# Out-projections chunk by chunk over each group of units in a two-layer mLSTM and gMLP trunk

## The chip, the cores and the metric

The kernel runs on the 8 cores of one Trainium2 chip. Two cores share a sequence of the batch: the even one takes the first 17 units of 128 tokens, the odd one the last 15. Time is device microseconds of the slowest core, the median of several executions. TensorE multiplies, VectorE (DVE), ScalarE (ACT) and GpSimd (POOL) do the rest, SyncE (SP) issues DMAs, as do ACT and POOL.

## The reference

`reference` runs two layers over x of shape (4, 4096, 2048), each with a residual add, and a last RMSNorm:

```python
xn = rmsnorm(h, mlstm_norm_g);  h = h + mlstm_layer(xn, ...)   # y @ w_out, y 4096 wide
xn = rmsnorm(h, gmlp_norm_g);   h = h + gmlp_layer(xn, ...)    # y @ w_out, y 4096 wide
return rmsnorm(h, final_norm_g)
```

The mLSTM layer projects to q, k, v, two gates and more, runs a chunked scan over 8 heads, norms and gates the result; the gMLP layer mixes tokens within chunks of 128. Both end in a product of (tokens x 4096) with (4096 x 2048), the out-projection, which is what the change touches.

## The kernel before

An even core (`PASSES_E`) takes its 17 units in passes of n = 9 and 8. An odd core (`PASSES_O`) first builds the scan's state out of the even core's tokens (`prefix`), then takes its 15 units in passes of 8 and 7. A pass is `phase_a` (projections, scan, by head), `phase_b` (out-projection `w0`, with the second layer's norm), `phase_cd` (gMLP up to the gate) and `phase_e` (out-projection `w1`, with the final norm, and with the first norm of the next pass's units among it).

**Weights.** `WQ` (class at L199 and on) has 5 slots (`NWSLOT`) of one chunk each: 8 x 128 rows by 512 columns, cast to bf16 by the DMA, which GpSimd issues (L218). `cur` hands out the slots of the next chunks, `done(k)` lets go of k chunks in their order, and each time issues the load of the next chunk that has none yet, that is five chunks further on. The issue waits on GpSimd's queue until TensorE has read the slot. An input projection takes 2 chunks (K = 2048), an out-projection 4 per column block `cb` (K = 4096), and there are 4 blocks of 512 columns.

**Order.** The code is written out in program order; each engine keeps to it. `sc.tick()` advances a counter, and `sc.defer(k, f)` has f written out at the k-th tick from now. A tick is thus a place in the order of TensorE's work, not a time.

**Out-projection** (`out_phase`). The units are split in g0 and g1 (4 and 4 for n = 8, 4 and 3 for n = 7). For each block and group, each unit of the group gets a PSUM bank out of a ring of 6 (`accr`) and the 16 matmuls of chunks 0 and 1; then each gets the 16 of chunks 2 and 3 and its `evict`. There is a tick behind every 16 matmuls. In g1 `done(2)` stands between the halves and again at the end. In blocks 0 to 2 `evict` adds the residual's tile (L1313; 5 tiles, loaded 4 ahead by SP), ScalarE squares it with a sum (L1286) and issues its DMA to `h_scr`. In block 3 the add (L1297) goes into a row of 2048 (4 rows in `w0`, 5 in `w1`), which `load_row` fills from `h_scr` and the residual in two DMAs (L193 and L1274), and then follow square, reduce (L1301), `rstd` on GpSimd (L509, L512) and `finish`.

`finish` of `phase_b` writes the row's last quarter to `h_scr`, defers `norm_scale` (L538, VectorE) by one tick and `norm_T` by three: 16 transposes on TensorE (L546) into banks PT and PS, which ScalarE (L551) and VectorE (L554) copy out. `finish` of `phase_e` defers the scale (L1509) and the row's output DMA by one. The row of unit s + 4 (or s + 5) is loaded a few ticks behind unit s's `evict`. `phase_cd` needs unit s's transposed norm at its projection of unit s (L649), `phase_a` starts with L631.

Of the kernel before, what the change touches and what calls it, by code (L numbers as in the profile page):

```python
# [279 lines left out]
def build_program():  # L280
# [32 lines left out]
    def emit(res, PREFIX, PASSES):  # L313
# [3 lines left out]
        sc = Sched()  # L317
# [931 lines left out]


        def out_phase(S, n, ub, key, res, resb, orow, finish):
# [26 lines left out]
            def mmg(ws, c0, s, pj, pjb, start, stop):  # L1278
                k = len(ws)
                tk.mm([lambda p, i=i: p.matmul(pj[:, :], lhsT=S.yt[:, c0 * 8 + i, s * 128:(s + 1) * 128],  # L1280
                                               rhs=ws[i // 8][0][:, i % 8, :], start=(start and i == 0),
                                               stop=(stop and i == 8 * k - 1)) for i in range(8 * k)],
                      reads=[w[1] for w in ws] + [S.ytb[(c0 * 8 + 4 * i) // 4][s] for i in range(2 * k)], writes=[pjb])
# [8 lines left out]
            def evict(cb, s, pj, pjb):  # L1292
                u = ub + s
                if cb == 3:
# [11 lines left out]
                    if s + len(orow) < n:  # L1306
                        sc.defer(len(orow) - 1, lambda: load_row(s + len(orow)))
# [14 lines left out]
            for cb in range(4):  # L1322
# [5 lines left out]
                for gi, g in enumerate((g0, g1)):  # L1328
                    for s in g:
                        open_[s] = accr.next()  # L1330
                        mmg(ws[0:2], 0, s, open_[s][0], open_[s][1], True, False)
                        sc.tick()
                    if gi == 1:
                        wq.done(2)
                    for s in g:
                        mmg(ws[2:4], 2, s, open_[s][0], open_[s][1], False, True)
                        evict(cb, s, *open_[s])
                        sc.tick()
                wq.done(2)

        def phase_b(S, n, ub):
# [4 lines left out]
            def finish(s, r, rb, k, ss):  # L1346
# [3 lines left out]
                sc.defer(1, lambda: norm_scale(ns, (r, rb), ss, s))  # L1350
                sc.defer(3, lambda: norm_T(ns, s, S.xt, s))
# [124 lines left out]
        def phase_e(S, n, ub, nxt):  # L1476
            ns = S.ns
            ns.gain = None
            if nxt is not None:
# [10 lines left out]
                def a2(s):  # L1490
                    st[s] = (st[s], norm_sq(ns, st[s], s))
# [4 lines left out]
                for s in range(n2):  # L1496
                    sc.defer(4 * s, lambda s=s: a1(s))
                    sc.defer(4 * s + 6, lambda s=s: a2(s))
                    sc.defer(4 * s + 7, lambda s=s: a3(s))
                    sc.defer(4 * s + 10, lambda s=s: norm_T(ns, s, S2.xt, s))  # L1500
                sc.defer(4 * n2 + 7, lambda: ns.set_gain(gfbc_d))
# [3 lines left out]
            def finish(s, r, rb, k, ss):  # L1505
# [8 lines left out]
                sc.defer(1, last_)  # L1514
# [91 lines left out]
```

How the kernel before makes its waits and increments, by code:

```python
    def wait(self, e, tk):  # L137
        if tk is None:
            return
        sem, val, key = tk
        if key == e and e == "pe":
            return
        if self.seen[e].get(key, 0) >= val:
            return
        self.eng[e].wait_ge(sem, val)
        self.seen[e][key] = val
# [23 lines left out]
    def op(self, e, fn, reads=(), writes=()):  # L170
        self._deps(e, reads, writes)
        ins = fn(self.eng[e])
        self.cnt[e] += 1
        ins.then_inc(self.sem[e], 1)
        tk = (self.sem[e], self.cnt[e], e)
        self._mark(tk, reads, writes)
        return tk
# [1 line left out]
    def mm(self, fns, reads=(), writes=()):  # L179
        e = "pe"
        self._deps(e, reads, writes)
        ins = None
        for fn in fns:
            ins = fn(self.eng[e])
        self.cnt[e] += 1
        ins.then_inc(self.sem[e], 1)
        tk = (self.sem[e], self.cnt[e], e)
        self._mark(tk, reads, writes)
        return tk
# [1 line left out]
    def dma(self, e, ds, out, in_, reads=(), writes=()):  # L191
        self._deps(e, reads, writes)
        self.eng[e].dma_start(out=out, in_=in_).then_inc(ds.sem, 16)
        ds.cnt += 16
        tk = (ds.sem, ds.cnt, ds.key)
        self._mark(tk, reads, writes)
        return tk
# [12 lines left out]
    def _load(self):  # L210
# [5 lines left out]
        tk._deps("pool", (), [b])  # L216
        for (co, ncol, src) in self.chunks[i][1]:
            tk.eng["pool"].dma_start(out=t[:, :, co:co + ncol], in_=src).then_inc(ds.sem, 16)
            ds.cnt += 16
```

## Time and profile before

| | us |
|---|---|
| median of 3 executions (lowest, highest) | 4827.49 (4821.77, 5116.9) |
| profiled execution, its own time | 4821.41 |
| its span, slowest core (7) | 4817.8 |
| spans of the odd cores | 4811.4 to 4817.8 |
| spans of the even cores | 4714.0 to 4716.9 |

The 3.6 us between the profiled execution's time and its span lie around the traced instructions. A row of a timeline gives the start, the duration, engine, source line, output and inputs, count, and in brackets the idle time before it with what ended it. Rows of equal instructions are merged; a merged row of matmuls overlaps the next by the drain of its last one.

### The profile page before, as it was taken

To read this page: it belongs to the slowest core of one execution; us is meant where nothing else is said; L and a number is where in the kernel's file an instruction comes from. 1 tells how busy PE (TensorE), PEld (TensorE's weight loads), DVE (VectorE), ACT (ScalarE), POOL (GpSimd) and SP (SyncE) were. 2 spreads that over 40 slices of the span, in tenths; PEclk is the share of its full clock that TensorE was granted. 3 is DMA by queue.
4 is the path that set the end of the run, shared out by engine and by line. 5 is a ranking of instruction groups with operands and counts; after the bars stand their busy time and mean duration, and the time that the engine had idled before them with its cause. 6 is when DMAs were issued, how large, how long until landed. Compare 5 with 4: busy or idle time off the path is not lost.

```text
span 4817.8 us, 70400 instructions; the slowest of 8 cores (4714.0 to 4817.8 us)
## 1 busy us (share of the span) xinstructions
PE 4616.2 (96%) x25992; PEld 2346.1 (49%) x25992; DVE 1639.2 (34%) x2973; ACT 1484.6 (31%) x2951; POOL 602.8 (13%) x843
## 2 busy tenths in 40 slices
PE   4899989999999999999999999999999999999998
PEld 3564445555555544444444445555555444455543
DVE  5571023443333420202444224444334211044312
ACT  5451023333333320342222213444333213322200
POOL 2000011111112110100000011212112100000000
PEclk9999999999999999999999999999999999999999
DMA  9454264554555458644554797565656686555577
GB/s 267 64 110 96 54 157 64 82 82 78 73 77 82 77 118 174 128 75 71 76 79 74 186 225 133 83 91 82 93 78 80 131 181 113 88 88 83 87 132 211
DMA packets 430603, 520.59 MB, mean 108 GB/s; under 512 B 14768, under 2 KB 375600, under 8 KB 423344
## 3 DMA queue, kind: packets, MB, share of 16 engines
q0 software_dynamic: 368144, 335.63, 48.2%
q1 hardware_dynamic: 44688, 148.65, 9.2%
q10 hardware_dynamic: 17424, 31.73, 1.9%
q8 instruction: 213, 3.49, 0.3%
q14 instruction: 134, 1.10, 0.1%
HBM read 791.01 MB, written 60.56 MB: 177 GB/s over the span
## 4 chain that ended last, share of the span: by engine, by line
PE 88%; DMA 7%; issue 2%; DVE 2%; ACT 1%; POOL 0%; SPq 0%; DVEq 0%; ACTq 0%; POOLq 0%
PE ps_PJ L649 30%; PE ps_PJ L1422 17%; PE ps_PJ L631 7%; PE ps_PJ L1280 6%; PE ps_PK L1280 5%; PE ps_PK L631 4%; DMA sb_w<-w_out 4%; PE ps_PK L649 3%; PE ps_PJ L876 2%; PE ps_PN L1280 2%; PE ps_PN L631 2%; DMA sb_w<-w_in 2%; PE ps_PK L876 1%; PE ps_PN L649 1%; PE ps_PN L1099 1%
## 5 line engine op out<-in xcount | busy, mean ns | idle before, releaser
L649 PE MATMUL ps_PJ<-sb_w,sb_xnT 128*128 128x512 bf16 x6720 | 1493.4, 379 | 14.7 <-DVE sb_scr L641 14.3
L649 PEld LDWEIGHTS ps_PJ<-sb_w,sb_xnT 128*128 128x128 bf16 x6720 | 650.0, 98 | 775.5 <-issue 20.0
L1422 PE MATMUL ps_PJ<-sb_xnT,sb_w 128*128 128x512 bf16 (+1 forms) x4096 | 850.3, 366 | 0.0
L1422 PEld LDWEIGHTS ps_PJ<-sb_xnT,sb_w 128*128 128x128 bf16 x4096 | 395.5, 98 | 402.3
L218 POOL DMA_DIRECT2D sb_w<-w_in x288 | 256.3, 896 | 2379.5 <-PE ps_PJ L649 576.9
L1280 PE MATMUL ps_PJ<-sb_w,sb_YT 128*128 128x512 bf16 x1920 | 426.3, 380 | 11.5 <-DMA sb_w<-w_out 11.5
L631 PE MATMUL ps_PJ<-sb_xnT,sb_w 128*128 128x388 bf16 (+1 forms) x1920 | 295.1, 311 | 31.8 <-DMA sb_w<-w_in 31.8
L1280 PE MATMUL ps_PK<-sb_w,sb_YT 128*128 128x512 bf16 x1280 | 291.5, 386 | 18.2 <-DMA sb_w<-w_out 18.2
L1280 PEld LDWEIGHTS ps_PJ<-sb_w,sb_YT 128*128 128x128 bf16 x1920 | 187.3, 98 | 238.1 <-issue 18.3
L1286 ACT ACTIVATE sb_scr<-sb_scr 128x512 bf16<-128x512 f32 x120 | 75.5, 630 | 737.1 <-DVE sb_scr L1313 533.6
L641 DVE SCALAR_TENSOR_TENSOR sb_scr<-ps_PJ,sb_convw,sb_scr 128x384 f32<-128x384 f32 (+1 forms) x432 | 245.0, 569 | 108.4 <-ACT sb_scr L636 50.2
L631 PEld LDWEIGHTS ps_PJ<-sb_xnT,sb_w 128*128 128x128 bf16 x1920 | 186.2, 98 | 119.6 <-issue 41.3
L1280 PEld LDWEIGHTS ps_PK<-sb_w,sb_YT 128*128 128x128 bf16 x1280 | 126.0, 99 | 173.6 <-issue 30.7
L1076 DVE SCALAR_TENSOR_TENSOR sb_scr<-ps_PS,sb_bk,sb_maskT 128x128 bf16<-128x128 f32 x120 | 42.0, 350 | 471.7 <-PE ps_PT L1082 468.4
L631 PE MATMUL ps_PK<-sb_xnT,sb_w 128*128 128x388 bf16 (+1 forms) x1280 | 194.0, 306 | 7.4 <-DMA sb_w<-w_in 7.4
L1118 DVE COPY sb_dnt<-ps_PS 128x3 f32<-128x3 f32 (+1 forms) x120 | 19.3, 161 | 470.3 <-PE ps_PS L1107 443.4
L641 DVE SCALAR_TENSOR_TENSOR sb_scr<-ps_PK,sb_convw,sb_scr 128x384 f32<-128x384 f32 (+1 forms) x288 | 160.4, 561 | 50.8 <-ACT sb_scr L636 27.5
L1159 POOL TENSOR_TENSOR sb_scr<-sb_scr 128x512 f32<-128x512 f32 x120 | 143.6, 1197 | 229.3 <-ACT sb_scr L1230 224.2
L1206 ACT ACTIVATE sb_scr<-ps_PJ 128x512 bf16<-128x512 f32 x120 | 71.7, 597 | 324.2 <-PE ps_PJ L649 324.2
L1448 ACT ACTIVATE sb_scr<-ps_PJ 128x512 bf16<-128x512 f32 (+1 forms) x128 | 73.0, 571 | 300.2 <-PE ps_PJ L1422 236.4
L1123 DVE SCALAR_TENSOR_TENSOR sb_scr<-sb_scr,sb_egt,ps_PK 128x512 f32<-128x512 f32 x224 | 157.5, 744 | 18.3 <-PE ps_PK L1113 4.0
L509 POOL TENSOR_TENSOR sb_sm<-sb_sm,sb_epst 128x1 f32<-128x1 f32 x182 | 42.5, 233 | 954.7 <-ACT sb_scr L1149 515.8
(206 smaller groups left out, 4890.1 us busy)
## 6 DMA issues: line engine op xcount, KB each, us to landing
sb_w<-w_in POOLq DMA_DIRECT2D x224, 1024.0 KB, 13.4
sb_w<-w_out POOLq DMA_DIRECT2D x64, 1024.0 KB, 14.6
sb_w<-w_in POOLq DMA_DIRECT2D x64, 512.0 KB, 11.5
h_scr<-sb_scr ACTq DMA_DIRECT2D x105, 256.0 KB, 6.2
sb_scr<-h_scr SPq DMA_DIRECT2D x30, 768.0 KB, 8.1
sb_YT<-xp SPq DMA_DIRECT2D x16, 1024.0 KB, 13.5
sb_scr<-xm SPq DMA_DIRECT2D x60, 256.0 KB, 5.6
sb_scr<-h_scr SPq DMA_DIRECT2D x60, 256.0 KB, 6.8
```

Source lines behind the costliest of these rows:

```text
L218: tk.eng["pool"].dma_start(out=t[:, :, co:co + ncol], in_=src).then_inc(ds.sem, 16)
L631: tk.mm([lambda p, kc=kc: p.matmul(pj[:, 0:n + 4], lhsT=wts[kc // 8][0][:, kc % 8, c0:c0 + 128], rhs=xt.ap[:, kc, t0:t0 + n + 4], start=(k ...
L641: tk.op("dve", lambda v, j=j: v.scalar_tensor_tensor(out=acc[:, 0:n], in0=pj[:, 1 + j:1 + j + n], scalar=convw[:, ch, j:j + 1], in1=acc[:, ...
L649: tk.mm([lambda p, kc=kc: p.matmul(pj[:, :], lhsT=xt.cols(kc, s), rhs=wts[kc // 8][0][:, kc % 8, :], start=(kc == 0), stop=(kc == KC - 1)) ...
L876: tk.mm([lambda p, k=k, u=u: p.matmul(pj[:, :], lhsT=xn(u)[0][:, i * 128:(i + 1) * 128], rhs=kw[:, j, u, :], start=(start and k == 0), sto ...
L1123: tk.op("dve", lambda v, cc=cc, PK=PK: v.scalar_tensor_tensor(out=C[:, cc, :], in0=C[:, cc, :], scalar=egt[:, c, h:h + 1], in1=PK[:, :], o ...
L1159: tk.op("pool", lambda g: g.tensor_tensor(out=hz, in0=S.hg[0], in1=sz, op=ALU.mult), reads=[szb, S.hg[1]], writes=[hzb])
L1206: tk.op("act", lambda a, s=s, pj=pj: a.activation(out=S.vt[:, s, :], in_=pj[:, :], func=AF.Copy), reads=[pjb], writes=[S.vtb[s]])
L1280: tk.mm([lambda p, i=i: p.matmul(pj[:, :], lhsT=S.yt[:, c0 * 8 + i, s * 128:(s + 1) * 128], rhs=ws[i // 8][0][:, i % 8, :], start=(start a ...
L1286: tk.op("act", lambda a: a.activation(out=S.sqj[0], in_=x, func=AF.Square, scale=D ** -0.5, accum_out=S.hsq[:, s, cb:cb + 1]), reads=[xb], ...
L1422: tk.mm([lambda p, kc=kc: p.matmul(pj[:, 0:m * 128], lhsT=wts[kc // 8][0][:, kc % 8, c0:c0 + 128], rhs=xt.cols(kc, u0, m), start=(kc == 0) ...
L1448: tk.op("act", lambda a, pj=pj, szt=szt, w=w: a.activation(out=szt[:, 0:w], in_=pj[:, 0:w], func=AF.Silu), reads=[pjb], writes=[sztb])
```

## The change

The four chunks of a block are gone through one by one over the whole group, with a tick behind every 8 matmuls, and in the last group each chunk is let go of behind its last unit. In block 3 the groups come from `groups(n)`: 3, 3, 3 for n = 9, else 4 and the rest, which for n = 8 and 7 are the groups as before. Deferrals that count ticks of the out-projection are doubled (`phase_e`), or set anew: in `phase_b` the norm steps of a unit in the last group keep 1 and 3 ticks, those of the i-th unit of another group are put 4 + i and 7 + i ticks behind its `evict`; a row is loaded anew 8 (`w0`) or 10 (`w1`) ticks behind the `evict` of the unit that had it.

```diff
+        def groups(n):
+
+            k = 4 if n < 9 else 3
+            return [list(range(a, min(a + k, n))) for a in range(0, n, k)]
...
-            def mmg(ws, c0, s, pj, pjb, start, stop):
-                k = len(ws)
+            def mmg(w, c0, s, pj, pjb):
                 tk.mm([lambda p, i=i: p.matmul(pj[:, :], lhsT=S.yt[:, c0 * 8 + i, s * 128:(s + 1) * 128],
-                                               rhs=ws[i // 8][0][:, i % 8, :], start=(start and i == 0),
-                                               stop=(stop and i == 8 * k - 1)) for i in range(8 * k)],
-                      reads=[w[1] for w in ws] + [S.ytb[(c0 * 8 + 4 * i) // 4][s] for i in range(2 * k)], writes=[pjb])
+                                               rhs=w[0][:, i, :], start=(c0 == 0 and i == 0),
+                                               stop=(c0 == 3 and i == 7)) for i in range(8)],
+                      reads=[w[1], S.ytb[2 * c0][s], S.ytb[2 * c0 + 1][s]], writes=[pjb])
...
-                        sc.defer(len(orow) - 1, lambda: load_row(s + len(orow)))
+                        sc.defer(2 * len(orow), lambda: load_row(s + len(orow)))
...
-                for gi, g in enumerate((g0, g1)):
-                    for s in g:
-                        open_[s] = accr.next()
-                        mmg(ws[0:2], 0, s, open_[s][0], open_[s][1], True, False)
-                        sc.tick()
-                    if gi == 1:
-                        wq.done(2)
-                    for s in g:
-                        mmg(ws[2:4], 2, s, open_[s][0], open_[s][1], False, True)
-                        evict(cb, s, *open_[s])
-                        sc.tick()
-                wq.done(2)
+                gs = groups(n) if cb == 3 else (g0, g1)
+                for g in gs:
+                    for c0 in range(4):
+                        for s in g:
+                            if c0 == 0:
+                                open_[s] = accr.next()
+                            mmg(ws[c0], c0, s, open_[s][0], open_[s][1])
+                            if c0 == 3:
+                                evict(cb, s, *open_[s])
+                            sc.tick()
+                        if g is gs[-1]:
+                            wq.done(1)
...
-                sc.defer(1, lambda: norm_scale(ns, (r, rb), ss, s))
-                sc.defer(3, lambda: norm_T(ns, s, S.xt, s))
+                gs = groups(n)
+                d = 0 if s in gs[-1] else 2 + [g.index(s) for g in gs if s in g][0]
+                sc.defer(2 + d if d else 1, lambda: norm_scale(ns, (r, rb), ss, s))
+                sc.defer(5 + d if d else 3, lambda: norm_T(ns, s, S.xt, s))
...
-                    sc.defer(4 * s, lambda s=s: a1(s))
-                    sc.defer(4 * s + 6, lambda s=s: a2(s))
-                    sc.defer(4 * s + 7, lambda s=s: a3(s))
-                    sc.defer(4 * s + 10, lambda s=s: norm_T(ns, s, S2.xt, s))
-                sc.defer(4 * n2 + 7, lambda: ns.set_gain(gfbc_d))
+                    sc.defer(8 * s, lambda s=s: a1(s))
+                    sc.defer(8 * s + 12, lambda s=s: a2(s))
+                    sc.defer(8 * s + 14, lambda s=s: a3(s))
+                    sc.defer(8 * s + 20, lambda s=s: norm_T(ns, s, S2.xt, s))
+                sc.defer(8 * n2 + 14, lambda: ns.set_gain(gfbc_d))
...
-                sc.defer(1, last_)
+                sc.defer(2, last_)
```

## Rows read from the trace of the kernel before

**Rows 1.** Spans of the cores: us, mean granted TensorE clock.

```profile
core 6: 4715.7 us, clock 0.994
...
core 7: 4817.8 us, clock 0.991
```

**Rows 2.** Page, part 1, TensorE: busy us, share, instructions.

```profile
PE 4616.2 (96%) x25992; PEld 2346.1 (49%) x25992; DVE 1639.2 (34%) x2973; ACT 1484.6 (31%) x2951; POOL 602.8 (13%) x843
```

**Rows 3.** Waits of TensorE on core 7: us in total, times, longest.

```profile
PE ps_PT L546 <- ACT sb_xnT L551: 18.6, 8, 4.2
...
PE ps_PK L1280 <- DMA sb_w<-w_out: 18.2, 7, 6.1
...
PE ps_PJ L1280 <- DMA sb_w<-w_out: 11.5, 8, 3.0
...
PE ps_PK L631 <- DMA sb_w<-w_in: 7.4, 1, 7.4
...
PE ps_PJ L649 <- DMA sb_w<-w_in: 0.4, 1, 0.4
```

**Rows 4.** Chain of waits in `w0` of pass 1: start us, us, what.

```profile
1852.23 13.82 DMA sb_w<-w_out
```

**Rows 5.** Timeline of GpSimd, end of the first `w1` phase.

```profile
2882.57 2.70 POOL L218 DMA_DIRECT2D sb_w<-w_in  x3 [5.47 <-PE ps_PN L1280]
```

**Rows 6.** Timeline of TensorE: usual groups, and groups behind waits for weights.

```profile
1900.71 10.52 PE L1280 MATMUL ps_PJ<-sb_w,sb_YT 128*128 128x512 bf16 x48
...
1926.78 3.62 PE L1280 MATMUL ps_PN<-sb_w,sb_YT 128*128 128x512 bf16 x16
...
2736.04 8.50 PE L1280 MATMUL ps_PK<-sb_w,sb_YT 128*128 128x512 bf16 x32 [6.07 <-DMA sb_w<-w_out]
...
2903.28 6.84 PE L631 MATMUL ps_PK<-sb_xnT,sb_w 128*128 128x388 bf16 x32 [7.45 <-DMA sb_w<-w_in]
...
3456.12 2.79 PE L631 MATMUL ps_PK<-sb_xnT,sb_w 128*128 128x388 bf16 x16
...
3834.35 5.30 PE L1280 MATMUL ps_PK<-sb_w,sb_YT 128*128 128x512 bf16 x16 [3.08 <-DMA sb_w<-w_out]
...
4647.98 6.49 PE L1280 MATMUL ps_PK<-sb_w,sb_YT 128*128 128x512 bf16 x16 [5.29 <-DMA sb_w<-w_out]
...
4718.22 12.21 PE L1280 MATMUL ps_PJ<-sb_w,sb_YT 128*128 128x512 bf16 x48 [2.96 <-DMA sb_w<-w_out]
```

**Rows 7.** Page, part 6: loads by count, KB each, median us to landing.

```profile
sb_w<-w_out POOLq DMA_DIRECT2D x64, 1024.0 KB, 14.6
...
sb_scr<-h_scr SPq DMA_DIRECT2D x30, 768.0 KB, 8.1
```

**Rows 8.** Waits of TensorE, around `w0` of pass 1, then of pass 2.

```profile
PE ps_PT L546 <- ACT sb_xnT L551: 5.2, 3, 2.6
...
PE ps_PT L546 <- ACT sb_xnT L551: 3.8, 2, 2.4
```

**Rows 9.** Timeline of all engines, last group of `w0` in pass 1.

```profile
1972.87 0.68 DVE L1297 TENSOR_TENSOR sb_scr<-ps_PJ,sb_scr 128x512 f32<-128x512 f32 x1
...
1975.47 0.61 PE L546 MATMUL ps_PT<-sb_ident,sb_scr 128*128 128x128 bf16 x8 [1.97 <-ACT sb_xnT L551]
...
1975.80 2.35 DVE L538 SCALAR_TENSOR_TENSOR sb_scr<-sb_scr,sb_sm 128x2048 bf16<-128x2048 f32 x1 [0.49 <-POOL sb_sm L512]
...
1978.07 0.68 DVE L1297 TENSOR_TENSOR sb_scr<-ps_PN,sb_scr 128x512 f32<-128x512 f32 x1
```

**Rows 10.** Timeline of TensorE, first group's norms of `w0`, pass 1.

```profile
1942.41 4.24 PE L1280 MATMUL ps_PJ<-sb_w,sb_YT 128*128 128x512 bf16 x16
```

**Rows 11.** Timeline of all engines, the end of the span.

```profile
4795.87 7.07 PE L1280 MATMUL ps_PJ<-sb_w,sb_YT 128*128 128x512 bf16 x32
...
4810.14 2.35 DVE L1509 SCALAR_TENSOR_TENSOR sb_scr<-sb_scr,sb_sm 128x2048 f32<-128x2048 f32 x1 [1.20 <-POOL sb_sm L512]
```

**Rows 12.** Timeline of TensorE, `phase_a`: two matmuls into banks PK0 and PK1.

```profile
1739.07 0.59 PE L1113 MATMUL ps_PK<-sb_scr 128*128 128x512 bf16 x2
```

## The prediction

> **What bounds the kernel now.** First the cores: the odd ones, which run the state scan and then passes of 8 and 7 units, last 4811 to 4818 us, the even ones (9 and 8 units) 4714 to 4717 [rows 1]. The time is core 7's, and an even core has 100 us to spare: all counts below are of core 7. Then the page's busy times: TensorE is busy 4616.2 of 4817.8 us [rows 2], so what can be had is mostly in its 200 us of idle time and what its clock loses after waits. Then TensorE's waits [rows 3]: in the out-projections (L1280) it waits 15 times for `w_out` chunks, 18.2 + 11.5 = 29.7 us; once, at the first block after the first `w1` phase, 7.4 us for `w_in`, and 0.4 us at another phase start; 18.6 us for transposes of the norms (L546 after L551), of which those behind `w0` are 5.2 + 3.8 us [rows 8]. The chain of waits shows why a chunk is late: after a column block it runs through a DMA of 13.82 us that began when GpSimd issued it at 1852.23 [rows 4], with a second one behind it, since `done(2)` lets go of two.
>
> **The order of the matmuls and the release of slots.** One chunk and unit is 8 matmuls. Their pace is (10.52 - 3.62) / 32 = 0.2156 us [rows 6], so a step of the new order is 1.73 us where the old one was 3.45. The count of matmuls, weight loads, evictions and DMAs does not change. With 5 slots, letting go of chunk k starts the load of chunk k + 5, which for chunk c of a block is chunk c + 1 of the next. Before, chunks 0 and 1 went together, halfway through the last group: 4 x 3.45 = 13.8 us ahead of the block's end for n = 8, 3 x 3.45 = 10.4 us for n = 7, and the very first matmul of the next block wanted the late one. A `w_out` chunk takes 14.6 us to land in the median [rows 7]. So every block boundary is a few us short, which is what the 15 waits say. After, chunk 0 goes at 3/4 of the last group still to come (20.7 us for n = 8, 15.5 for n = 7) and its successor is wanted a full step row later (4 x 1.73 = 6.9 us into the next block): 27.6 and 22.5 us of lead. Chunk 2 of the next block gets 13.8 + 13.8 = 27.6 (n = 7: 10.4 + 13.8 = 24.2), chunk 3 gets 6.9 + 20.7 = 27.6 (n = 7: 5.2 + 20.7 = 25.9). The worst landing read off the waits is 13.8 + 6.1 = 19.9 us for n = 8 and 10.4 + 5.3 = 15.7 for n = 7; all leads are longer. At a phase's first block the chunk that used to be wanted 13.8 us in is now wanted 20.7 us in. Bounds: all 29.7 us go, or, if bursts of evictions and row loads push landings to 28 us, some 10 stay. I take 2 left: 27.7 gained.
>
> **The clock behind these waits.** Behind five of them the granted clock falls to its lower level for a stretch, seen as longer rows of the same count [rows 6]: 8.50 against 7.07 us for 32 matmuls, 5.30 against 3.62 and 6.49 against 3.62 for 16, 12.21 against 10.52 for 48, and at L631 6.84 where 32 matmuls of that width take 2 x 2.79 less the overlap of 0.16 that each group of 16 has with the next (3.62 against 3.45), 5.4. That is 1.4 + 1.7 + 2.9 + 1.7 + 1.4 = 9.1 us, and it goes with the waits.
>
> **The next phase's first weights.** The 7.4 us stood before chunk 1 of the first block of pass 2, issued at 2882.57 behind half of the last group, with two more transfers [rows 5], and landed at 2903.3: 20.7 us. It is now issued 20.7 us ahead of the end instead of 13.8, alone. Bounds: 6.9 us gained, or all 7.4 with less company in the queue. I take 6.9, and 0.4 at the other start, 7.3. What is queued behind a waiting release on GpSimd is `rstd` of later units; in block 3 the releases now lie between groups of evictions, and the last one still comes behind the last unit's `rstd`, as before, but holds one chunk that is wanted late, where it held two.
>
> Sum of gains: 27.7 + 9.1 + 7.3 = 44.1 us.
>
> **The norm steps in block 3 of `w0`.** One unit's chain on VectorE, from add (L1297) through ScalarE's square, reduce, GpSimd's two steps and the scale (L538, 2.35 us) to the next unit's add, takes 1978.07 - 1972.87 = 5.2 us [rows 9], because the scale is put right behind the evict and holds up the next add. TensorE's tick was 3.45 us, now it is 1.73. For the first group the scales are put off by 4 ticks and more and spaced by two (3.46 us, for a scale of 2.35 us and a short copy): its waits, 2.6 us in pass 1 and 2.4 in pass 2 [rows 8], and the clock behind them, about 1.5 us in each pass (an estimate from the row of 4.24 us where 3.62 is usual [rows 10] and the transposes ahead of it) go. For the last group the distance is unchanged in ticks and halved in time. With e the end of its first unit: the add starts at about e + 0.15, the scale ends 1975.80 + 2.35 - 1972.87 = 5.3 us later, and the first transpose can run at e + 5.6 and TensorE is there at e + 3.45: waits 2.2. The second is put behind ScalarE's copy of the first, which is behind the third unit's square; by rows 9 it comes 1975.47 - 1972.87 = 2.6 us after the third add, which is at e + 0.15 + 2 x 5.3 = e + 10.7: e + 13.3. For n = 8 TensorE is there at e + 8.2 (waits 5.1), for n = 7, one projection of the next phase later, at e + 10.0 (waits 3.3). The third in n = 8 waits 0.8, the fourth nothing. With about 2 us of clock behind each: 10.1 and 7.2 us, 17.3 together, against 9.0 of waits [rows 8] and 3 of clock now. That is 5.3 us lost. Bounds: 0 (VectorE's chain shortens, since its squares wait less) to 12 (row loads late as well: for n = 7 a row is now reloaded 5 ticks and some transposes, about 11 us, ahead of its add, and 768 KB land in 8.1 [rows 7]).
>
> **Evictions.** In blocks 0 to 2 four adds come 1.73 us apart instead of 3.45, then a pause of 20.7 us. An add is 0.68 us, a bank is wanted again five steps (8.6 us) after its last matmul, and the residual tiles of a group are loaded in the pause: hidden. If that cover went, each group would pay the excess over 8.6 us.
>
> **Phase `w1`.** Its ticks for the next pass's norms are doubled, which leaves their times where they were: 0. In block 3 the scale comes two ticks behind, so adds of two units lie closer. At the very end: TensorE ends at 4795.87 + 7.07 = 4802.9, the last scale at 4812.5 [rows 11], the span 5.3 us later. After, three units must be finished from 3.3 us before TensorE's end; a unit costs VectorE 5.2 us less the 1.20 that the scale waited for GpSimd [rows 11], now covered by the next unit's add, 4.0; so it would end 12.0 - 3.3 = 8.7 us behind TensorE, against 9.6 now. But rows 5 and 6 are reloaded 10 ticks behind their forerunners, only 4 ticks = 6.9 us before their adds, and take 8.1 [rows 7]: some 1.5 us late. Bounds -0.5 to +4; I take +1.
>
> **Sum.** -44.1 + 5.3 + 1 = -37.8 us, on a span of 4817.8 and a time of the profiled execution of 4821.4: 4783.6. The median shown, 4827.5, lies 6 above that execution, so the same gain from it gives 4789.7. I take 4787, -0.8%.
>
> **A rule weighed.** A group now goes to another PSUM bank every 8 matmuls instead of every 16, 240 more changes of bank on core 7 (30 unit-phases x 4 blocks x 2). The row of L1113 has two matmuls into two different banks, 0.59 us together [rows 12], so the second starts about 0.21 us behind the first: a change of bank costs nothing that shows.
> The Trainium skill, "TensorE: Matmul & The Clock Gate", section "A second HAM failure mode: psum-queue depth-cycling", says that cycling through banks let TensorE pause briefly between groups so often that its clock went up and down and throughput fell. By that rule this change would be slower (rival 2); the trace does not agree so far, since groups of 16 follow each other without a gap at the upper of the two levels.
>
> **Rivals.** (1) The waits move instead of going. For: DMA is shared by weights, rows, residuals and outputs, and in block 3 the rows' loads now come 1.73 us apart. Against: leads are 22 us and more. Half of 27.7 + 9.1 stays, and the end effects take 8: -(18.4 + 7.3) + 8 = -17.7, 4807. (2) TensorE pays for each change of bank. With one matmul's 0.2156 us for each of 240 it is 51.7 us, so -37.8 + 51.7 = +13.9: 4838, slower. It decides from 37.8 / 240 = 0.16 us per change. Against it stands rows 12. (3) The last group's norms do not wait as reckoned, because the scheduler's new delays let the adds run ahead, and all waits for weights go: -46 - 9, 4770. (4) Nothing changes: the odd cores are held by something that refills the time, 4825. Nothing in the waits speaks for it.
>
> **How the numbers follow.** Forecast 0.60 (4774 to 4800), rival 1 0.20, rival 3 0.10, rival 2 0.05, rival 4 0.05. The range that leaves out half of rival 3 and most of 2 and 4 is 4767 to 4818. A measurement of this kernel can tell about 2% from no change (4731 or 4924): faster by over 2% would need 97 us of 200 idle, 0.01; slower by over 2%, 0.01; within, 0.98.
>
> **What would show it.** Right: TensorE's waits for `w_out` under 5 us in total; the `w_in` wait of 7.4 gone; the transposes behind `w0` waiting 13 us in all, with the longest about 5 in the last group of pass 1 and none in the first groups; GpSimd's weight issues one by one, 6.9 and 5.2 us apart; TensorE's last matmul to span end 15 to 16 us. Wrong: waits of L1280 for a DMA of over 10 us, waits of L1280 for an add (a bank), or steps of 8 matmuls that take more than 1.73 us without a wait.

## The result, and the profile after

The changed kernel takes 0.9939 of the time of the kernel before (95% interval 0.9911 to 0.9968), so it is 0.6% faster, less than the 2% that a measurement of this kernel is taken to tell from no change; the lowest times are 4793.6 and 4821.7 us. Executions in which one die's cores show a lower granted clock are left out here, and of the experiments `best` and `unspaced` only cores 5 and 7 are read. The profiled execution took 4795.25 us against the 4783.6 that was worked out for it: 26.2 us gained of 37.8. The odd cores still set the time:

```profile
core 5: 4791.5 us, clock 0.991
...
core 6: 4684.9 us, clock 0.996
core 7: 4790.3 us, clock 0.991
```

Core 7 went from 4817.8 to 4790.3 us, 27.5 us, and all that follows is read there. Its page, part 1:

```profile
PE 4613.1 (96%) x25992; PEld 2347.6 (49%) x25992; DVE 1638.9 (34%) x2973; ACT 1488.3 (31%) x2951; POOL 628.0 (13%) x843
```

The counts are those of [rows 2]. TensorE is 3.1 us less busy (it runs fewer matmuls at the lower clock) and mostly less idle. GpSimd does the same 843 instructions in 25.2 us more, 21.2 of them in L509; that comes back below. Then the waits of TensorE on core 7 (us in total, times, longest), which answer to [rows 3]:

```profile
PE ps_PJ L631 <- DMA sb_w<-w_in: 32.1, 2, 26.7
...
PE ps_PT L546 <- ACT sb_xnT L551: 11.6, 5, 3.2
...
PE ps_PK L631 <- DMA sb_w<-w_in: 6.6, 1, 6.6
PE ps_PT L546 <- DVE sb_scr L538: 6.4, 4, 2.3
...
PE ps_PJ L649 <- DMA sb_w<-w_in: 3.0, 1, 3.0
...
PE ps_PN L1284 <- DVE sb_YT L1142: 0.9, 1, 0.9
PE ps_PJ L1284 <- DMA sb_w<-w_out: 0.9, 1, 0.9
```

The 15 waits for `w_out` (29.7 us) have become one of 0.9, and cores 1, 3 and 5 have none. The wait at the first block of pass 2 (`ps_PK L631`) did not go: 6.6 us where it was 7.4 (5.1 to 5.4 on cores 1, 3 and 5), and 3.0 more at the first matmuls of L649 soon after. The 32.1 us of `ps_PJ L631` are in the prefix, ahead of all that was changed. The matmuls of `w0` in the new order, on TensorE's timeline (start us, us, instruction, count):

```profile
1751.90 1.89 PE L1284 MATMUL ps_PJ<-sb_w,sb_YT 128*128 128x512 bf16 x8
1753.62 1.89 PE L1284 MATMUL ps_PN<-sb_w,sb_YT 128*128 128x512 bf16 x8
1755.35 3.62 PE L1284 MATMUL ps_PK<-sb_w,sb_YT 128*128 128x512 bf16 x16
1758.80 1.89 PE L1284 MATMUL ps_PJ<-sb_w,sb_YT 128*128 128x512 bf16 x8
```

Starts lie 1.72 to 1.73 us apart for each 8 matmuls, through every change of bank: the pace of [rows 6], with nothing added.

A table by stage shows where the time went (core 7, us). The stage of `w0` begins with its first matmul and ends behind the last transposes of its norms, which stand among the first projections of `phase_cd`; the chunk work, which is the rest of `phase_cd`, ends with the first matmul of `w1`, and a pass ends with the first matmul of the next.

| stage | before | after | difference |
|---|---|---|---|
| `w0` of pass 1 | 246.2 | 247.1 | +0.9 |
| chunk work, then `w1` of pass 1 | 672.1 + 245.2 | 672.1 + 234.0 | -11.2 |
| pass 2 up to `w0` | 877.9 | 880.2 | +2.3 |
| `w0` of pass 2 | 223.1 | 215.1 | -8.0 |
| chunk work, then `w1` of pass 2 | 588.1 + 210.5 | 588.1 + 193.6 | -16.9 |
| last matmul to the span's end | 14.9 | 17.0 | +2.1 |

With 3.3 us by which `w0` of pass 1 began later (1739.7, then 1743.0) these give -27.5, as the spans do. The 193.6 us of `w1` in pass 2 are 896 matmuls (7 units, 4 blocks, 4 chunks of 8) at 0.2161 us, the pace with no wait at all: nothing is left to gain there.

The norm steps of `w0` in pass 1 on TensorE's timeline, after:

```profile
1944.65 0.61 PE L546 MATMUL ps_PT<-sb_ident,sb_scr 128*128 128x128 bf16 x8 [0.93 <-DVE sb_scr L538]
...
1971.40 0.61 PE L546 MATMUL ps_PT<-sb_ident,sb_scr 128*128 128x128 bf16 x8 [2.29 <-DVE sb_scr L538]
1971.85 0.84 PE L546 MATMUL ps_PS<-sb_ident,sb_scr 128*128 128x128 bf16 x8
1972.48 3.38 PE L1284 MATMUL ps_PN<-sb_w,sb_YT 128*128 128x512 bf16 x8
...
1978.88 1.01 PE L546 MATMUL ps_PT<-sb_ident,sb_scr 128*128 128x128 bf16 x8 [3.02 <-ACT sb_xnT L551]
```

The first row is of the first group, the others of the last. In the last group the waits are where they were forecast: 2.29 us ahead of its first transposes, then 3.02 ahead of the second. Between the two, 8 matmuls run at the lower clock, 3.38 us where 1.89 is usual; they end later, and TensorE then waits that much less. The 0.93 in the first group was not forecast.

### The profile page after: what moved, and what is told of

Its sections match the earlier page's. It is cut to its first block, busy times and chain, and to the rows that moved or that the text cites. A ratio compares the mean times of both kernels' runs of the same rounds, so it can differ in the third digit from the quotient of the medians.

```text
span 4791.5 us, 70451 instructions; the slowest of 8 cores (4676.7 to 4791.5 us)
## 1 busy us (share of the span) xinstructions
PE 4612.1 (96%) x25992; PEld 2346.1 (49%) x25992; DVE 1638.3 (34%) x2973; ACT 1485.1 (31%) x2951; POOL 631.4 (13%) x843
## 4 chain that ended last, share of the span: by engine, by line
PE 91%; DMA 3%; DVE 2%; issue 2%; ACT 1%; POOL 0%; SPq 0%; DVEq 0%; ACTq 0%; POOLq 0%
PE ps_PJ L649 30%; PE ps_PJ L1428 17%; PE ps_PJ L1284 8%; PE ps_PJ L631 6%; PE ps_PK L1284 5%; PE ps_PK L631 4%; PE ps_PK L649 3%; PE ps_PN L1284 3%; PE ps_PJ L876 2%; DMA sb_w<-w_in 2%; PE ps_PN L631 2%; PE ps_PK L876 1%; PE ps_PN L649 1%; PE ps_PN L1099 1%; PE ps_PK L1113 1%
## 5 line engine op out<-in xcount | busy, mean ns | idle before, releaser
L649 PE MATMUL ps_PJ<-sb_w,sb_xnT 128*128 128x512 bf16 x6720 | 1496.8, 380 | 15.5 <-DVE sb_scr L641 12.9
L649 PEld LDWEIGHTS ps_PJ<-sb_w,sb_xnT 128*128 128x128 bf16 x6720 | 650.8, 98 | 778.7 <-issue 25.1
L1284 PE MATMUL ps_PJ<-sb_w,sb_YT 128*128 128x512 bf16 x1920 | 433.3, 379 | 0.0
L631 PE MATMUL ps_PJ<-sb_xnT,sb_w 128*128 128x388 bf16 (+1 forms) x1920 | 295.4, 311 | 32.9 <-DMA sb_w<-w_in 32.9
L1284 PEld LDWEIGHTS ps_PJ<-sb_w,sb_YT 128*128 128x128 bf16 x1920 | 187.3, 98 | 223.2
L1284 PE MATMUL ps_PK<-sb_w,sb_YT 128*128 128x512 bf16 x1280 | 291.6, 379 | 0.0
L641 DVE SCALAR_TENSOR_TENSOR sb_scr<-ps_PJ,sb_convw,sb_scr 128x384 f32<-128x384 f32 (+1 forms) x432 | 244.6, 569 | 106.1 <-ACT sb_scr L636 51.2
L631 PEld LDWEIGHTS ps_PJ<-sb_xnT,sb_w 128*128 128x128 bf16 x1920 | 186.0, 98 | 120.8 <-issue 42.6
L631 PE MATMUL ps_PK<-sb_xnT,sb_w 128*128 128x388 bf16 (+1 forms) x1280 | 194.0, 306 | 5.1 <-DMA sb_w<-w_in 5.1
L1284 PEld LDWEIGHTS ps_PK<-sb_w,sb_YT 128*128 128x128 bf16 x1280 | 124.9, 98 | 148.6
L509 POOL TENSOR_TENSOR sb_sm<-sb_sm,sb_epst 128x1 f32<-128x1 f32 x182 | 67.2, 369 | 911.6 <-ACT sb_scr L1149 513.7
L641 DVE SCALAR_TENSOR_TENSOR sb_scr<-ps_PK,sb_convw,sb_scr 128x384 f32<-128x384 f32 (+1 forms) x288 | 160.3, 560 | 44.9 <-ACT sb_scr L636 22.0
## 6 DMA issues: line engine op xcount, KB each, us to landing
sb_YT<-xp SPq DMA_DIRECT2D x16, 1024.0 KB, 11.9
```

The lines of the kernel that those rows point to most:

```text
L631: tk.mm([lambda p, kc=kc: p.matmul(pj[:, 0:n + 4], lhsT=wts[kc // 8][0][:, kc % 8, c0:c0 + 128], rhs=xt.ap[:, kc, t0:t0 + n + 4], start=(k ...
L641: tk.op("dve", lambda v, j=j: v.scalar_tensor_tensor(out=acc[:, 0:n], in0=pj[:, 1 + j:1 + j + n], scalar=convw[:, ch, j:j + 1], in1=acc[:, ...
L649: tk.mm([lambda p, kc=kc: p.matmul(pj[:, :], lhsT=xt.cols(kc, s), rhs=wts[kc // 8][0][:, kc % 8, :], start=(kc == 0), stop=(kc == KC - 1)) ...
```

## The experiments

**The same kernel once more (`again`).**

> The changed kernel once more, as the measure for the others of this job, and for the 3.3 us by which the stretch ahead of the first w0 phase, which the change does not touch, came out longer on core 7 (first w0 matmul at 1743.0 us instead of 1739.7). Theory chance: the first w0 matmul of the odd cores lies anywhere from 1736 to 1745 us from one execution to the next. Rival code placement: it is again at 1743 within 1 us on core 7. Time 4790 to 4798 us.

Measured: odd cores 4791.5, 4787.8, 4788.1 and 4790.9 us, stages of core 7 within 1.1 us of the table's, and `w0` of pass 1 begins at 1745.4 on core 7. Over the odd cores of all runs here that start lies between 1737.5 and 1750.2 us, with the same code ahead of it. The 3.3 us lie within this spread. The means of the four odd cores are 1740.8 and 1742.5 in the two profiles of the kernel before, 1743.8 and 1744.1 in those of the changed one, so a shift of 2 us that belongs to the change isn't excluded. A difference of one run's span under some 5 us says nothing; stages do, since they begin behind it.

**Order or release (`pairs`).** The new order of matmuls, but two slots let go of together, as before.

```diff
-                        if g is gs[-1]:
-                            wq.done(1)
+                        if g is gs[-1] and c0 % 2:
+                            wq.done(2)
```

> Order by chunk as changed, but chunks are let go of in twos behind chunk 1 and chunk 3 of the last group, at the times of the kernel before. Theory A (a chunk is wanted later, that is what pays): leads are 20.7 us for n = 8 and 17.3 us for n = 7, landings 15 to 20 us, so TensorE's waits for w_out stay under 3 us on an odd core, and the time is at most 4 us over the changed kernel's. Theory B (the early single release pays): half of the 29.7 us of waits is back and part of the clock with it, time 15 to 20 us over the changed kernel's. Either way the w_in wait at the start of pass 2 is some 3 us longer at most, since its chunk is issued later.

Measured: 0.9934 (0.9911 to 0.9956), the changed kernel's ratio. TensorE waits for no `w_out` chunk on any odd core, core 7's stages of the out-projections are 247.7, 234.4, 214.1 and 193.6 us, and the wait for `w_in` at pass 2 is 7.0. The release times here are those of before (the slots of chunks 0 and 1 go halfway through the last group), so the gain is the order's: chunks 1 and 3 of a block are first wanted 6.9 us later. These are the two that TensorE waited for before. For each of the 15 waits the trace has the position in its block and the landing of the chunk that ended it. Four waits, 10.5 us, stand ahead of a block's first matmul, all in pass 2, where the last group has 3 units: there chunk 1 is late. The other eleven, 19.2 us, stand 64 matmuls into a block, where the first unit turns to chunks 2 and 3: there chunk 3 is late, the load that goes out only behind the end of the block before. The other odd cores have 9.6 to 11.9 us of the first kind and 11.8 to 15.8 of the second. The longest, the 6.07 us of [rows 6], is of this kind (TensorE, then GpSimd, kernel before):

```profile
2715.10 7.07 PE L1280 MATMUL ps_PK<-sb_w,sb_YT 128*128 128x512 bf16 x32
...
2715.81 1.81 POOL L218 DMA_DIRECT2D sb_w<-w_out  x2 [2.77 <-PE ps_PN L1280]
```

The block begins at 2715.10 without a wait, chunk 3 is issued at 2715.81 and lands at 2735.9, and TensorE goes on at 2736.04. In the new order, that each slot is let go of by itself gives nothing that can be seen, neither between blocks nor at the start of pass 2.

**Other distances for the norm steps (`normticks`, `late`, `best`, `unspaced`).** Four kernels, each with the deferrals of `phase_b` (scale, transposes) set otherwise.

```diff
# normticks
-                sc.defer(2 + d if d else 1, lambda: norm_scale(ns, (r, rb), ss, s))
-                sc.defer(5 + d if d else 3, lambda: norm_T(ns, s, S.xt, s))
+                sc.defer(2, lambda: norm_scale(ns, (r, rb), ss, s))
+                sc.defer(6, lambda: norm_T(ns, s, S.xt, s))
# late
+                sc.defer(2 + d if d else 2, lambda: norm_scale(ns, (r, rb), ss, s))
+                sc.defer(5 + d if d else 5, lambda: norm_T(ns, s, S.xt, s))
```

> Norm steps of w0 at 2 and 6 ticks of half the length for every unit: the places in TensorE's time that they had before the change. Theory A (the new delays are worth having because they take the first group's steps apart): the first groups' transposes wait again, 2 to 3 us each pass plus about 1.5 us of clock, the last group's wait less by 2 to 4 us each pass, so the time is within 5 us of the changed kernel's. Rival (they carry much of the gain): 10 us or more slower than the changed kernel.

> In the last group of w0 the scale comes 2 ticks and the transposes 5 ticks behind the evict, where it was 1 and 3. Theory A (what stands behind w0 is the scale that holds up the next unit's add, 5.2 us a unit): adds run ahead of scales, transposes come behind a projection each, waits of L546 in the last groups go from 8.9 us in the two passes of core 7 to under 1, and the clock behind them stays up: 10 to 14 us faster than the changed kernel. Rival (the projections of phase_cd then wait for the norms, or ScalarE's copies behind its Gelus hold them): waits of L649 for L551 or L554 appear in their place and the time is within 4 us of the changed kernel's.

Both change a part of the computation: there are two buffers for normed rows, and with transposes 4 (`normticks`) or 3 (`late`, in the last group only) ticks behind a scale, the scale of unit s + 2 is put ahead of the transposes of unit s and writes its row over that one's, so TensorE transposes the later row, and waits for it. `normticks` came to 0.995 (0.993 to 0.997), lowest time 4802.2 us, 8.6 above the changed kernel's; `late` to spans of 4783.8 to 4794.5 us on the odd cores. From the start of `w0` to the start of `w1` they take 921.4 and 917.9 us in pass 1 and 804.2 and 805.0 in pass 2, against 919.2 and 803.2 of the changed kernel. Most of what `normticks` loses on core 7 lies behind that: `w1` of pass 1 and pass 2 up to `w0` take 1119.6 us (changed kernel 1114.2), with a wait of 14.2 us for `w_in`; why that load came so late was not followed. `normticks` has a wait of 6.9 us at the first group, `late` one of 6.0 in the last:

```profile
1979.79 1.01 PE L546 MATMUL ps_PT<-sb_ident,sb_scr 128*128 128x128 bf16 x8 [6.04 <-ACT sb_scr L1373]
```

They test a distance and an overwritten buffer at once, so neither settles what the distance is worth. Mended, with the transposes two ticks behind the scale (the next but one scale is then put behind them), and with the row reloads of `w1` 5 ticks behind instead of 10:

```diff
# best
-                        sc.defer(2 * len(orow), lambda: load_row(s + len(orow)))
+                        sc.defer(8 if key == "w0" else 5, lambda: load_row(s + len(orow)))
...
+                sc.defer(2 + d if d else 2, lambda: norm_scale(ns, (r, rb), ss, s))
+                sc.defer(5 + d if d else 4, lambda: norm_T(ns, s, S.xt, s))
# unspaced: the row reloads as in the changed kernel, and for every unit of every group
+                sc.defer(2, lambda: norm_scale(ns, (r, rb), ss, s))
+                sc.defer(4, lambda: norm_T(ns, s, S.xt, s))
```

> Two edits that fall into stages of their own. In the last group of w0 the scale comes 2 and the transposes 4 ticks behind the evict (two buffers are then enough), and in w1 a row is loaded again 5 ticks behind its forerunner's evict instead of 10. From the start of the first w0 to the start of the first w1 on core 7, now 919.2 to 919.8 us, theory A (the scale right behind the evict is what holds the norms) expects 911 to 913, in pass 2 797 to 799 instead of 803; rival (phase_cd is held instead) no less than 918 and 802. Behind the last matmul the span now goes on for 17.0 us: if the late row of unit 5 is what holds it, 15.5; if it is GpSimd's steps beside VectorE's scale, 16.5 or more. Time 10 to 14 us under the changed kernel's by theory A.

> Scale 2 and transposes 4 ticks behind the evict for every unit of w0, so the first group's steps are not set apart. Theory A (setting them apart pays): VectorE needs 2.35 us and more for a unit and a tick is 1.73, so the first group's transposes wait, 3 us or more in each pass, and the stretch from w0 to w1 is 3 to 6 us longer in each pass than in best. Rival: the transposes come out even and the stretch is within 1 us of best's.

Both change one thing in what the even cores compute: unit 8's scale now comes inside the chunk work, where scratch of ScalarE overlays its row. `best` measured 0.9912 (0.9892 to 0.9931), and its lowest time, 4790.8 us, is 2.8 below the changed kernel's, where 10 to 14 were expected. Start of `w0` to start of `w1` is 914.7 us on core 7 and 913.8 on core 5 in pass 1 (changed kernel 919.2 and 919.7), 806.4 and 800.0 in pass 2 (803.2 and 802.2). From last matmul to span end it is 15.3 us, not 17.0 (16.2 to 17.0 over all odd cores of the changed kernel's two profiles), and the add of unit 5 no longer waits for its row. So the stretch of pass 1 came out 1 to 4 us over what theory A expected, and that of pass 2 did not follow it. In `unspaced` the same stretch is 923.7 and 920.5 us in pass 1, and 803.4 and 805.3 in pass 2. Its first group in pass 1, on TensorE's timeline:

```profile
1939.29 0.61 PE L546 MATMUL ps_PT<-sb_ident,sb_scr 128*128 128x128 bf16 x8 [2.17 <-DVE sb_scr L538]
...
1945.76 1.01 PE L546 MATMUL ps_PT<-sb_ident,sb_scr 128*128 128x128 bf16 x8 [3.70 <-ACT sb_xnT L551]
```

`unspaced` differs from `best` in the row reloads of `w1` too, but those lie outside the stretches compared. So of the norm steps two things are shown, for pass 1 alone. Spacing the scales of the first group pays 9.0 us on core 7 and 6.7 on core 5 in pass 1; in pass 2 it is -3.0 and 5.3, unclear. And in the last group one tick more ahead of the scale and of the transposes takes 4.5 us (core 7) and 5.9 us (core 5) off pass 1; in pass 2 it is +3.2 and -2.2, unclear too.

**Why the first block of pass 2 still waits (`norowpart`, `scaleback`).** GpSimd's timeline at the end of the first `w1`, changed kernel:

```profile
2859.03 0.18 POOL L509 TENSOR_TENSOR sb_sm<-sb_sm,sb_epst 128x1 f32<-128x1 f32 x1 [22.31 <-DVE sb_sm L1305]
...
2860.87 2.34 POOL L509 TENSOR_TENSOR sb_sm<-sb_sm,sb_epst 128x1 f32<-128x1 f32 x1 [0.94 <-DVE sb_sm L1305]
...
2869.14 2.27 POOL L509 TENSOR_TENSOR sb_sm<-sb_sm,sb_epst 128x1 f32<-128x1 f32 x1 [1.14 <-DVE sb_sm L1305]
2871.56 0.55 POOL L512 TENSOR_TENSOR sb_sm<-sb_sm,sb_mhalf 128x1 f32<-128x1 f32 x1
2872.11 1.81 POOL L218 DMA_DIRECT2D sb_w<-w_in  x2
```

By the order of the matmuls the slot was free at 2868.8 (12 steps of 1.73 us ahead of the last matmul's end at 2889.5; its drain ends at 2889.7), but the issue stood behind `rstd` of the fourth unit and came at 2872.11: 3.3 us late, still 10.5 earlier than the 2882.57 of [rows 5] (of which 6.1 are the whole phase, which ended earlier). Yet the chunk landed at 2896.3, after 24.2 us instead of 20.7. What it met, in the DMA view of the 36 us from 10 us ahead of the issue (KB each, median us to landing), changed kernel:

```profile
DMA  0079902994069904998999999999999999999999
...
out<-sb_scr SPq DMA_DIRECT2D x6, 1024.0 KB, 6.0
sb_scr<-h_scr SPq DMA_DIRECT2D x3, 768.0 KB, 13.5
...
sb_w<-w_in POOLq DMA_DIRECT2D x2, 512.0 KB, 18.4
```

and on SP's queue:

```profile
2863.24 11.80 SPq L193 DMA_DIRECT2D out<-sb_scr  x4
2875.13 1.68 SPq L193 DMA_DIRECT2D sb_scr<-h_scr  x1
2876.86 0.96 SPq L1279 DMA_DIRECT2D sb_scr<-h_scr  x1
2877.90 0.96 SPq L193 DMA_DIRECT2D sb_scr<-h_scr  x1
```

Four outputs of 1 MB are issued from SP's queue between 2863.2 and 2875.1, and the reloads of three rows behind them, until 2880.8: all three behind the weight's issue at 2872.11. The same view of the kernel before, from 2868 on (there all three reloads are issued between 2874.8 and 2883.2, up to the weight's issue at 2882.57):

```profile
DMA  0099700099979999989997999999999999999999
...
sb_scr<-h_scr SPq DMA_DIRECT2D x3, 768.0 KB, 7.9
sb_w<-w_in POOLq DMA_DIRECT2D x2, 512.0 KB, 15.9
```

The first line is the busy share of the 16 DMA engines in tenths, in 40 slices: full behind the issue in both kernels, and the same pieces land later in the changed one. The first experiment leaves those 768 KB out in `w1` (rows beyond the first set in `w1` are then not the residual's but what the buffer held):

```diff
-                    tk.eng["sp"].dma_start(out=r[:, 0:1536], in_=Hd[u * 128:(u + 1) * 128, 0:1536]).then_inc(ds.sem, 16)
-                    ds.cnt += 16
+                    if key == "w0" or s < len(orow):
+                        tk.eng["sp"].dma_start(out=r[:, 0:1536], in_=Hd[u * 128:(u + 1) * 128, 0:1536]).then_inc(ds.sem, 16)
+                        ds.cnt += 16
```

> The 768 KB of each reloaded row in w1 are left out (units 5 to 7, and 5 and 6 in the last pass), so three quarters of those rows are not the residual. Theory A (the first weights of pass 2 are late because the DMA engines are full): 2.3 MB less ahead of them, so the wait of L631 falls from 5.9 to 7.0 us to under 2 and the L649 wait of 1.8 to 3.0 goes. Rival (they are late because GpSimd issues them late, behind its steps beside VectorE's scale): the wait stays at 5 us or more.

Measured: the wait of 6.6 is gone on core 7 (none on cores 3 and 5, 1.7 us on core 1). The second piece of that chunk lands 15.7 to 18.1 us behind its issue on the four odd cores, where the changed kernel has 21.5 to 23.0, and it is issued no more than 1.1 us earlier against the phase's end. So the wait is there because of what the reloads take of the DMA engines, and not because of when GpSimd issues the load. But TensorE's timeline then shows (lines from L1280 on are one higher in this kernel):

```profile
2891.34 5.42 PE L631 MATMUL ps_PK<-sb_xnT,sb_w 128*128 128x388 bf16 x32
...
2906.11 3.90 PE L631 MATMUL ps_PK<-sb_xnT,sb_w 128*128 128x260 bf16 x32 [0.55 <-DVE sb_scr L641]
...
2922.98 6.05 PE L649 MATMUL ps_PJ<-sb_w,sb_xnT 128*128 128x512 bf16 x16 [5.49 <-DVE sb_scr L641]
```

And VectorE's:

```profile
2901.64 2.35 DVE L1516 SCALAR_TENSOR_TENSOR sb_scr<-sb_scr,sb_sm 128x2048 f32<-128x2048 f32 x1 [0.91 <-POOL sb_sm L512]
2903.91 4.02 DVE L641 SCALAR_TENSOR_TENSOR sb_scr<-ps_PK,sb_convw,sb_scr 128x384 f32<-128x384 f32 x6
```

VectorE is done with the last scale of `w1` only at 2904, 12.6 us behind the first matmul of pass 2, and its convolution steps (L641) start behind it; TensorE has to wait 5.5 us for those instead. `w1` of pass 1 and pass 2 up to `w0` take 1112.7 us together, the changed kernel 1114.2 and, run again, 1112.4. Over all four odd cores it is 1111.3 to 1113.1 for 1112.2 to 1114.7: the whole cure of the DMA is worth 2 us at most in any core, and nothing on core 7 by the second profile. It had a second wait behind it. The one execution took 4803.6 us, which is more than the changed kernel: on its slowest core, 3, `w0` began late (1750.2), and from `w0` to `w1` both passes took some 3 and 4 us longer (922.5 and 806.6), which was not followed. The other experiment puts the last scale back to one tick:

```diff
-                sc.defer(2, last_)
+                sc.defer(1, last_)
```

> The scale of w1's last block stands one tick behind the evict instead of two. Theory A (with one tick, nothing of VectorE runs beside GpSimd's two steps, so L509 takes 0.19 us again where it now takes 2.3, but a unit's chain is 5.2 us long instead of 4.1): the span goes on for 19 to 21 us behind the last matmul instead of 17.0, and the issue of pass 2's first chunk on GpSimd comes later still, so the w_in wait grows by 2 to 4 us. Rival (GpSimd's slow step is what costs): the tail shortens below 16 us.

Measured: L509 takes 0.19 us again at the end of both `w1`, the first chunk of pass 2 is issued at 2877.82, three together, and is waited for 8.2 us, 1.6 more than in the changed kernel (1.9 to 3.9 more on the other odd cores); from last matmul to span end it is 20.1 us on all four, and the one execution took 4807.5. One unit costs VectorE 5.28 us again, since a scale waits for its own `rstd` with nothing between. The two ticks are worth 3.1 us at the end of the span even with the slow L509 (20.1 less 17.0; 3.6 to 3.9 on the other odd cores), and 1.3 in `w1` of pass 1 and pass 2 up to `w0` together (1115.5 less 1114.2; 2.1 to 3.7 on the others).

**The best version (`best2`).** `best`, with that scratch of ScalarE moved onto another buffer:

```diff
-            S.junk1 = ld.get("junk1", [512], BF16)
+            S.junk1 = S.sqj
```

> As best, with ScalarE's scratch of phase_cd laid over the square's scratch, so that it no longer lies over a row that is still to be scaled on the even cores. On core 7 the stretches of best again within 2 us where no DMA wait differs: w0 to w1 914 to 916 us in pass 1 (changed kernel 919.5), 800 to 806 in pass 2, 15.3 us behind the last matmul. Theory A (the stalls behind w0 stand partly in front of the wait for phase_cd's first chunk, so taking them away gives back some of it): time 4 to 8 us under the changed kernel's 4794. Rival (each stage's gain adds up): 12 us under it.

Measured: 0.9917 (0.99 to 0.9935), spans of the odd cores 4788.6, 4786.2, 4785.5 and 4780.3 us. Start of `w0` to start of `w1` takes 913.7 us on all four odd cores in pass 1 (changed kernel 919.2 to 919.8) and 804.0, 803.9, 800.5 and 798.0 on cores 1, 3, 5 and 7 in pass 2 (802.2, and 803.2 on core 7); last matmul to span end is 15.5 us. Of this 2.6 us are given back at pass 2 on core 7, where `w1` and pass 2 up to `w0` take 1116.8 us (1.8 to 1.9 on the other three), with this row:

```profile
2893.27 8.11 PE L631 MATMUL ps_PK<-sb_xnT,sb_w 128*128 128x388 bf16 x32 [9.47 <-DVE sb_scr L1515]
```

The wait is put down to a scale; cores 1, 3 and 5 wait 8.5, 6.5 and 6.2 us for `w_in` in that place. By the landings in the trace it is the weight on core 7 too: there the chunk's second piece landed at 2893.05, 0.2 us ahead of the matmul, and on the other three 0.2 to 0.3 us ahead. Its lowest time is 4788.6 us, 5.0 below the changed kernel's, and the slowest core's span 2.9 below; the intervals of the two ratios overlap, so the times alone don't show that it is faster than the changed kernel. What the stages show is 6 us in pass 1, with about 2 given back at pass 2 and a pass 2 that goes either way.

**The kernel before, once more (`before2`).**

> The kernel before, profiled once more, to see how far its stages move by themselves on the odd cores: first w0 matmul anywhere from 1736 to 1748 us, stage of w1 pass 1 242 to 247 us, of w1 pass 2 207 to 211, w_out waits 24 to 31 us. If instead the w_out waits are under 20 us, the 29.7 us of the first profile were a bad draw and the change gains less than they say.

Measured: odd cores 4818.5 to 4827.2 us, waits for `w_out` of 29.7, 34.6, 30.1 and 29.1 us, stages of core 7 within 1.8 us of the table's. Core 3's 34.6 is over the 24 to 31 expected. The 29.7 us are no accident of one run.

## Why the prediction came out as it did

The forecast was 0.8% faster, and it is 0.6%; the time lies in the range. Of the mechanism named, an earlier release and a later want, the later want did it alone, and one term, the first weights of pass 2, failed. The terms, on core 7, in the order of the prediction:

| term | forecast | measured |
|---|---|---|
| waits for `w_out` | -27.7 | -28.8 |
| clock behind them | -7.7 | -7.7 |
| first weights of pass 2, with their clock | -8.7 | +2.5 |
| norm steps of `w0` | +5.3 | +3.7 |
| the end | +1 | +2.1 |
| wait for `sb_YT` (L1142): `w0` now goes from unit to unit in 1.73 us | 0 | +0.9 |
| start of `w0`, within its spread | 0 | +3.3 |
| sum | -37.8 | -24.0 |

The span says -27.5; the 3.5 us between were not followed.

**Order and release.** The size is right, one reading behind it is not. The prediction had every block boundary short, with the very first matmul wanting the late chunk; that holds for four of the 15 waits, and the other eleven stood 64 matmuls further on, for chunk 3. Nothing was lost by it: the leads were worked out for chunk 3 too, and the longest landing read off the waits, 13.8 + 6.1, is the same for either chunk. Landings were also taken to stay under 20 us. In the trace of before a chunk 3 took 22.9 us, and in the changed kernel one took 26.1 us and landed 0.1 us before it was wanted, and one 22.6, which is the wait of 0.9 that stays where 2 us in all were taken. So leads of 22 to 27 us are enough here, but with little to spare. `pairs` adds what the prediction left open: it counted both an earlier release and a later want, and in this order the later want alone does it. How much single releases would have given without the new order was not run. Rival 1 (the waits move, 4807) fell for `w_out`, and holds in small for `w_in`.

**The clock.** Right: the four longer rows at L1280 are gone.

**The first weights of pass 2: the step that failed.** The prediction took the landing time of before (20.7 us) as given and moved its start by 6.9 us. It had the chunk issued 20.7 us ahead of the phase's end; it was 17.6 (2872.11, TensorE idle from 2889.7), for 13.3 before (2882.57, idle from 2895.8), since it stood behind the `rstd` of the fourth unit. Of the 4.3 us won in this way 3.5 were lost in the landing, 24.2 for 20.7. So the lower bound was missing: that nothing is gained. And "alone" was the wrong way to look at it: the DMA engines were full already, with outputs and row reloads around this load in either kernel, and in the changed one all three reloads come behind its issue. Behind the first chunk a second wait appeared (3.0 us), and the clock was low for longer (7.46 us for the 6.84 of [rows 6], where 5.4 is usual: 6.6 + 2.1 + 3.0 = 11.7 against 7.4 + 1.4 + 0.4). `norowpart` shows that even without all this VectorE's backlog would have taken 5.5 of it, so that no more than 2 us was to be had here.

**The norm steps.** Right in kind, and somewhat too dear: +5.3 forecast, +3.7 measured. The waits in the last groups are 2.29 and 3.02, then 2.30 and 1.32 us, where 2.2, 5.1 (and 0.8), then 2.2 and 3.3 were worked out; the first groups, from which none was expected, wait 0.93 and 0.89. The rows beside them that are longer than usual, counted from start to start, add 5.0; together 15.7, for 12.1 before (9.0 of waits and 3.1 of such rows). The second waits came out short where TensorE ran at its lower level between the two: it got there later and waited less. Without such rows the second wait is 4.70 us (pass 1, cores 1, 3 and 5, and core 7 of `pairs`) and 2.98 (pass 2, core 5), close to the 5.1 and 3.3. Either way the second transposes begin 7.48 to 7.49 us behind the first, on all four odd cores and in both passes. Of waits in a chain on another engine only the last end counts, and a loss of clock between two of them costs nothing.

**The end.** The sum of 8.7 + 1.5 us for VectorE's end behind TensorE was 11.8 (4785.1 less 4773.3). The rows that came late are there, and by `best` they are worth 1.0 to 1.7 us (cores 5 and 7), where 1.5 were reckoned. The rest is a thing that none of the rows read before showed, on the timeline of all engines:

```profile
4772.34 0.19 POOL L509 TENSOR_TENSOR sb_sm<-sb_sm,sb_epst 128x1 f32<-128x1 f32 x1 [9.72 <-DVE sb_sm L1305]
...
4773.55 0.69 DVE L1301 TENSOR_TENSOR sb_scr<-ps_PJ,sb_scr 128x512 f32<-128x512 f32 x1 [1.35 <-DMA sb_scr<-h_scr]
...
4779.48 2.35 DVE L1515 SCALAR_TENSOR_TENSOR sb_scr<-sb_scr,sb_sm 128x2048 f32<-128x2048 f32 x1
4779.61 2.27 POOL L509 TENSOR_TENSOR sb_sm<-sb_sm,sb_epst 128x1 f32<-128x1 f32 x1 [1.13 <-DVE sb_sm L1305]
4782.03 0.55 POOL L512 TENSOR_TENSOR sb_sm<-sb_sm,sb_mhalf 128x1 f32<-128x1 f32 x1
4782.75 2.35 DVE L1515 SCALAR_TENSOR_TENSOR sb_scr<-sb_scr,sb_sm 128x2048 f32<-128x2048 f32 x1 [0.91 <-POOL sb_sm L512]
```

With the scale put off, the `rstd` of the next unit falls beside it, and L509 takes 2.27 us instead of 0.19. The last unit's scale waits for that: 0.91 us in which VectorE is idle. On the other odd cores, and on all four in `again`, the end takes 16.2 to 16.5 us, so of the 2.1 here about 0.6 is this run's own. It was also taken that a unit costs 4.0 us there; the rows give 4.1 (4779.48 - 4775.38).

**Evictions and banks.** Right: no wait of L1284 for an add, and no pause at a change of bank. Rival 2 fell: 8 matmuls keep their 1.73 us through each of 240 more changes, and a whole phase of them takes 193.6 us. The rule of the Trainium skill that was weighed (page "TensorE: Matmul & The Clock Gate", section "A second HAM failure mode: psum-queue depth-cycling") does not show here: the granted clock of core 7 is 0.991, as it was before.

**The other marks.** `w_out` under 5 us: yes. The `w_in` wait gone: no. Transposes waiting 13 us behind `w0`, the longest about 5, none in the first groups: 10.7, the longest 3.0, 0.9 in each first group. GpSimd's issues 6.9 us apart: yes (1890.74, 1897.64, 1904.55, 1911.46). Last matmul to span end 15 to 16: 17.0, no.

## What to carry to other kernels

When weights are streamed through a few slots, ask first when the order of the loops first wants a chunk; that moved 29 us here, and with the new order in place, letting go of slots one by one moved nothing. Find for each wait which chunk ended it: here most waits were not at the block's start, where they were looked for. A transfer that is issued earlier does not land earlier by as much when the DMA engines are full: read the load of the stretch that it is moved into, and what the engine behind the wait (here VectorE) would be late with next, and let "nothing" be one end of the range. In a chain of waits on one other engine, count to the end of the chain; a loss of clock between two of the waits is not added.

## What was not expected of the hardware

A GpSimd add of 128x1 takes 0.19 us alone and 2.27 to 2.34 us when it starts just behind the start of a VectorE SCALAR_TENSOR_TENSOR of 128x2048 in f32 that takes 2.35 us (11 times on core 7): it ends when that ends, 0.05 us later in the rows of the end (4779.48 + 2.35 = 4781.83; 4779.61 + 2.27 = 4781.88). Over the kernel the 182 instructions of L509 go from 42.5 to 63.7 us on core 7, and in `scaleback`, with the two apart, those of the last block are at 0.19 again. The kernel before has the same thing in its prefix, where it was overlooked: five adds of L509 beside the scale of L538 take 0.85 to 2.31 us there. Beside the adds of L1301, which read one of their two inputs from PSUM, six of them keep 0.19 us. The VectorE instruction reads both of its tensors, the row and the gain, from SBUF. The Trainium skill's "GPSIMD Engine Reference", section "1. Specifications", says that the two engines share their SBUF interfaces and contend when the VectorE instruction reads two SBUF inputs; the rows agree, and here the small instruction loses all that is left of the large one.
